# Seven block products in place of eight in both feed-forward parts of a decoder layer

## What is computed

```python
x = x + 1/2 * swiglu(rmsnorm(x), w_gate, w_up, w_down)      # FFN 1
x = x + token_mix(rmsnorm(x))                               # projections, two recurrent mixers, output
x = x + memory_attention(rmsnorm(x), rmsnorm(mem))          # 4 heads over 256 memory tokens
x = x + 1/2 * swiglu(rmsnorm(x), w_gate, w_up, w_down)      # FFN 2
out = rmsnorm(x)
# swiglu(h) = (silu(h @ w_gate) * (h @ w_up)) @ w_down
```

## Time and profile before

| | us |
|---|---|
| runs, median (lowest) | 2969.23 (2969.01) |
| profiled execution, first to last instruction (its own time as the page gives it) | 2967.3 |
| PE busy | 2849.2 (96%) |
| DVE busy | 1354.6 (46%) |
| POOL busy | 1246.7 (42%) |
| ACT busy | 564.3 (19%) |

### The profile page before, as it was taken

One profiled execution on the slowest core, in us unless ns is written; L12 is line 12 of the kernel. 1 busy time (PEld: TensorE's weight loads), 2 busy tenths in 40 slices (PEclk: granted clock), 3 DMA queues, 4 the chain that ended last, 5 costly groups with the idle time before them and its releaser, 6 DMA issues.

```text
span 2967.3 us, 36791 instructions
## 1 busy us (share of the span) xinstructions
PE 2849.2 (96%) x14694; PEld 2359.7 (80%) x14694; DVE 1354.6 (46%) x1109; ACT 564.3 (19%) x793; POOL 1246.7 (42%) x627
## 2 busy tenths in 40 slices
PE   7999999999999998999999999998899999999996
PEld 5888888888788877777777778888788888888885
DVE  5431331234556535776777555543344322331334
ACT  3100010012000112443444232214321100100011
POOL 3433344433694623555555443321043344433331
PEclk9999999999999999998999999999999999999998
DMA  3111111112762554444434164122011111111111
GB/s 133 43 50 50 50 49 45 48 46 103 298 247 92 192 194 149 101 107 139 102 102 104 61 223 149 51 75 102 8 43 50 49 50 47 46 49 50 50 41 73
DMA packets 115401, 271.35 MB, mean 91 GB/s; under 512 B 7644, under 2 KB 58972, under 8 KB 108272
## 3 DMA queue, kind: packets, MB, share of 16 engines
q1 hardware_dynamic: 93504, 210.79, 22.4%
q10 hardware_dynamic: 21808, 59.27, 5.3%
HBM read 207.56 MB, written 62.44 MB: 91 GB/s over the span
## 4 chain that ended last, share of the span: by engine, by line
PE 79%; issue 9%; POOL 6%; DVE 4%; ACT 1%; DMA 0%; SPq 0%; POOLq 0%; DVEq 0%; ACTq 0%
PE G L755 24%; PE G L757 24%; PE G L756 24%; PE G L879 2%; POOL AL L686 2%; PE G L1164 1%; PE G L916 1%; POOL Tr L680 1%; ACT sx L1559 0%; DVE nt_a L1644 0%; DVE mx L2008 0%; DVE px L2016 0%; POOL rho L669 0%; PE G L1156 0%; PE G L820 0%
## 5 line engine op out<-in xcount | busy, mean ns | idle before, releaser
L719 POOL TENSOR_TENSOR whi<-raw,zero 128x1024 fp32r<-128x1024 f32 (+1 forms) x199 | 378.2, 1900 | 1312.8 <-PE G L757 1233.2
L755 PE MATMUL G<-hhi,whi 128*128 128x512 f32 x2032 | 794.0, 391 | 21.0 <-DVE hlo L1650 17.9
L757 PE MATMUL G<-hhi,wlo 128*128 128x512 f32 x2032 | 791.8, 390 | 0.0
L756 PE MATMUL G<-hlo,whi 128*128 128x512 f32 x2032 | 791.5, 390 | 0.0
L722 POOL TENSOR_TENSOR wlo<-raw,whi 128x1024 fp32r<-128x1024 f32 (+1 forms) x199 | 482.6, 2425 | 15.6
L755 PEld LDWEIGHTS G<-hhi,whi 128*128 128x128 f32 x2032 | 382.1, 188 | 104.2 <-issue 13.0
L757 PEld LDWEIGHTS G<-hhi,wlo 128*128 128x128 f32 x2032 | 382.1, 188 | 79.8
L756 PEld LDWEIGHTS G<-hlo,whi 128*128 128x128 f32 x2032 | 382.2, 188 | 79.6 <-issue 0.7
L755 PE MATMUL G<-ahi,whi 128*128 128x512 f32 x960 | 374.8, 390 | 2.7 <-DVEq L457 2.7
L756 PE MATMUL G<-alo,whi 128*128 128x512 f32 x960 | 374.2, 390 | 0.0
L757 PE MATMUL G<-ahi,wlo 128*128 128x512 f32 x960 | 374.1, 390 | 0.0
(11 more groups left out here) (329 smaller groups left out, 3301.8 us busy)
## 6 DMA issues: line engine op xcount, KB each, us to landing
gw<-gw_d SPq DMA_DIRECT2D x32, 1024.0 KB, 5.3
raw<-in_wg SPq DMA_DIRECT2D x44, 512.0 KB, 3.2
raw<-in_wu SPq DMA_DIRECT2D x44, 512.0 KB, 3.3
raw<-in_wd SPq DMA_DIRECT2D x32, 512.0 KB, 3.3
gw_d<-gw SPq DMA_DIRECT2D x16, 1024.0 KB, 4.8
graw<-in_gates_in SPq DMA_DIRECT2D x16, 512.0 KB, 7.2
raw<-in_ml_in SPq DMA_DIRECT2D x16, 512.0 KB, 3.7
zml_d<-po ACTq DMA_DIRECT2D x16, 512.0 KB, 2.6
```

The lines of the kernel that those rows point to most:

```text
L719: nc.gpsimd.tensor_tensor(whi[:, k, 0:w], raw[:, k, 0:w], zero[:].to_broadcast([P, w]), ALU.add).then_inc(hi_made, 1)
L755: nc.tensor.matmul(dst, wh, hi, start=start, stop=False)
L756: nc.tensor.matmul(dst, wh, lo, start=False, stop=False)
L757: return nc.tensor.matmul(dst, wl, hi, start=False, stop=stop)
```

## The change

The product of each feed-forward matrix is cut in 2x2 blocks and taken as seven block products with sums of blocks (a scheme of Strassen's kind) in place of eight.

- **Gate and up.** A unit is now a 256x1024 pair of columns: 11 gate and 11 up units per FFN, each of seven products ("ops") of 4 weight tiles by 512 tokens, 12 matmuls. The seven token operands of FFN entry (`tok`, four blocks or sums of `xT` halves, high and low) are made once and stay on chip. The weight operands are two raw blocks, four sums S1 to S4 and one raw block; POOL makes the four sums and the seven low parts, ACT the seven high parts, through a ring of four slots. ACT copies two partial outputs of a unit out of PSUM (`snap`, `both`); DVE combines the outputs in five steps (C11, v, C22, C12, C21), then scales, and after silu scales again (`gate`, `regate`) and multiplies (`tile`). SP stores finished activations to DRAM (`act_d`).
- **Down.** Product by product in the order 2, 4, 5, 3, 1, 7, 6, each over 11 row pairs (77 ops of 12 matmuls). For an op SP loads one or two weight blocks and, for the first four products, a block of activations from DRAM; POOL adds two weight blocks where the product has a sum (products 1, 2, 5, 6, 7), DVE adds two activation blocks (products 1, 3, 4, 6, 7), ACT makes both high parts, DVE both low parts; DVE also adds finished products onto `xT` (48 results of 128x512), which is loaded again from DRAM, since its place serves as buffer during gate and up.
- **Entry and exit.** Token sums on DVE from copies by ACT; the sum of squares is added on POOL in FFN 1 and on DVE in FFN 2. On exit the squares of even chunks are added by POOL, those of odd ones by DVE.

The diff, cut to its core. The sizes and orders:

```diff
-FF_PARTS = (8, 8, 6)
+FP = FFC // 2
+GU_OPS = 2 * FP * 7
+DN_OPS = 7 * FP
+RING = 4
+GU_WEIGHTS = ("11", "12", "S1", "S2", "S3", "S4", "22")
+DN_ORDER = (2, 4, 5, 3, 1, 7, 6)
+DN_LAG = 15
```

SP, loads and stores of an FFN:

```diff
+        def ffn_io(f):
...
+            for u in range(2 * FP):
+                load_pair(u)
+                if u > 1 and u % 2:
+                    store_tiles((u - 3) // 2)
...
+            for s in range(2 * RING, DN_OPS):
+                load_down(s)
+                p, j = divmod(s - 2 * RING, FP)
+                if p < 3:
+                    sp.wait_ge(dt_lo, f * DN_OPS + s - 2 * RING + 1)
+                    load_block(p + 1, j)
...
+        ffn_io(0)
+        sp.wait_ge(dn_lo, DN_OPS)
         for names, n, tiles, first, u0 in runs():
```

POOL, gate and up, and the first units after FFN 1:

```diff
+            for u in range(2 * FP):
+                low(u, 0)
+                total("S1", u)
+                low(u, 1)
+                total("S2", u)
+                total("S3", u)
+                low(u, 2)
+                total("S4", u)
+                for i in (3, 4, 5):
+                    low(u, i)
+                if f == 0 and u == 0:
+                    for k in range(4):
+                        add_in(k)
+                low(u, 6)
+                if f == 0 and u == 0:
+                    for k in range(4, KD):
+                        add_in(k)
...
+                    if u0 == 0:
+                        pool.wait_ge(op_used, FF_OPS - 5 if r == 0 else FF_OPS)
+                    if u0 == 0 and r == 1:
+                        add_out(0)
                     split(u % 2, i * rounds + u, i + (u // 2 + 1 - aside))
```

PE, one gate or up unit:

```diff
+            for i, bank in enumerate((A, B, C, A, E, B, E)):
+                o = 7 * u + i
+                pe.wait_ge(gu_lo, f * GU_OPS + o + 1)
...
+                if i == 5:
+                    pe.wait_ge(*gu_dve.at("C11", it))
+                if i == 6:
+                    pe.wait_ge(*gu_dve.at("C22", it))
```

ACT, entry to FFN 1:

```diff
+            if f == 0:
...
+                after(1)
+                for k in range(4):
+                    token_square(k)
+                after(2)
+                for k in range(4, KD):
+                    token_square(k)
+                act.wait_ge(in_add, KD + 1)
...
+            for j in range(JP):
+                token_hi(6, j)
```

ACT, exit:

```diff
+            for k in range(0, KD, 2):
+                if gain:
+                    act.dma_start(x_park[:, k, :], xT[:, k, :]).then_inc(store, 16)
+                    activation(hhi[:, k, :], xT[:, k, :], ACT.Copy, scale=v1(gain, k)).then_inc(*out_hi.sig(f"{k}"))
+                square(k)
```

DVE, gate and up:

```diff
+            for u in range(2, 2 * FP):
+                m = u // 2
+                evac("C11", u)
+                evac("v", u)
+                if u % 2:
+                    regate(m, 0)
+                evac("C22", u)
+                if u % 2:
+                    regate(m, 1)
+                evac("C12", u)
+                (tile if u % 2 else gate)(m, 0)
+                evac("C21", u)
+                (tile if u % 2 else gate)(m, 1)
```

DVE, down:

```diff
+            for s in range(DN_OPS):
+                act_sum(s + 1)
+                o = GU_OPS + s
+                dve.wait_ge(op_hi, O + o + 1)
+                tt(ring(wlo, f, o), weight_source(f, o), ring(whi, f, o).bitcast(F32), ALU.subtract).then_inc(dn_lo, 1)
...
+                tt(dtok[:, s % RING, 1, :], src, dtok[:, s % RING, 0, :].bitcast(F32), ALU.subtract).then_inc(dt_lo, 1)
+                if given < len(results) and s >= FP * results[given][0] + DN_LAG:
+                    result(given)
+                    given += 1
```

More of the change, by code:

```diff
@@ new lines, in down @@
+        def down(f, p):
+            for j in range(FP):
+                s = FP * p + j
+                o = GU_OPS + s
+                if j == 0 and p < 2:
+                    pe.wait_ge(*gu_dve.at("C21", f * 2 * FP + 2 * FP - 2 + p))
+                pe.wait_ge(dn_lo, f * DN_OPS + s + 1)
+                pe.wait_ge(dt_lo, f * DN_OPS + s + 1)
+                hi, lo = ring(whi, f, o), ring(wlo, f, o)
+                th, tl = dtok[:, s % RING, 0, :], dtok[:, s % RING, 1, :]
+                for n in range(KD // 2):
+                    if j == 0 and p >= 2:
+                        used = len(DN_OUT[DN_ORDER[p - 2]])
+                        pe.wait_ge(down_out, f * results_before(7) + results_before(p - 2) + used * (n + 1))
+                    bank = down_bank(p, n)
+                    wh, wl = hi[:, n * P:(n + 1) * P], lo[:, n * P:(n + 1) * P]
+                    nc.tensor.matmul(bank, wh, th, start=j == 0, stop=False, skip_group_check=True)
+                    nc.tensor.matmul(bank, wh, tl, start=False, stop=False, skip_group_check=True)
+                    last = nc.tensor.matmul(bank, wl, th, start=False, stop=j == FP - 1, skip_group_check=True)
+                last.then_inc(op_used, 1)
@@ new lines, in ffn, with exit_chunk, exit_norm @@
+        def ffn(f):
+            gate_up(f, 0)
+            pe.wait_ge(consts_in, CONSTS * 16)
+            pe.wait_ge(in_add, (f + 1) * (KD + 1))
+            ones_product(G[1], nt_b[:])
+            for u in range(1, 2 * FP):
+                gate_up(f, u)
+            for p in range(7):
+                down(f, p)
+        def exit_chunk(t):
+            pe.wait_ge(*out_lo.at(f"{t}b" if t % 2 else f"{t}", 0))
+        def exit_norm(f):
+            pe.wait_ge(*out_odd.at("7", f))
+            dve_bank(c.dve)
+            ones_product(bank_dve(c.dve), nt_x[:])
+            c.dve += 1
@@ L1214, in _ @@
         gemm(KD, "dve", hi=ahi, lo=alo)
-        ffn(nt_b[:])
-        norm(nt_b[:], T)
+        ffn(1)
+        exit_norm(1)
     @block.scalar
@@ L1673, in residual @@
             c.advance(unit=KD, dve=KD)
-        def partial(scale):
-            with loop(dve, KD // 2) as i:
-                for r in range(2):
-                    output_ready(i * 2 + (c.unit + r))
-                    x_ = xT[:, i * 2 + r, :]
-                    stt(x_, flat(bank_dve(c.dve + r)[:]), scale, x_, ALU.mult, ALU.add).then_inc(dve_free, 1)
-            c.advance(unit=KD, dve=KD)
         def norm_root(width, ms, r, t):
@@ new lines, in leave, with low @@
+        def leave(f, gain, result):
+            def low(name, k, h0, h1):
+                dve.wait_ge(*out_hi.at(name, 0))
+                stt(hlo[:, k, h0:h1], xT[:, k, h0:h1], v1(gain, k), hhi[:, k, h0:h1].bitcast(F32), ALU.mult,
+                    ALU.subtract).then_inc(*out_lo.sig(name))
+            dve.wait_ge(dt_sum, (f + 1) * sums_before(DN_T, DN_OPS))
+            if gain:
+                for k in range(0, KD, 2):
+                    low(f"{k}", k, 0, T)
+                for k in range(1, KD, 2):
+                    low(f"{k}a", k, 0, HALF)
+            done = results_before(6)
+            result(done)
+            for n in range(1, KD // 2):
+                result(done + n)
+                if gain:
+                    low(f"{2 * n - 1}b", 2 * n - 1, HALF, T)
+            if gain:
+                low(f"{KD - 1}b", KD - 1, HALF, T)
+            for k in range(1, KD, 2):
+                dve.wait_ge(*out_sq.at(f"{k}", f))
+                dve.wait_ge(*(out_odd.at(f"{k - 2}", f) if k > 1 else out_even.at(f"{KD - 2}", f)))
+                tt(nt_x[:], nt_x[:], sqx[:, OUT_SQ.index(f"{k}") % 2, :], ALU.add).then_inc(*out_odd.sig(f"{k}"))
@@ L2146, with quarters @@
     arrays = {}
+    def quarters(w):
+        k, n = w.shape[0] // (2 * P), w.shape[1] // (2 * P)
+        return w.reshape(k, 2, P, n, 2, P)
+    gate_up, down = [], []
     for f in ("ffn1", "ffn2"):
-        n = f[-1]
-        arrays[f"wg{n}"] = units(g[f"{f}_w_gate"][0])
-        arrays[f"wu{n}"] = units(g[f"{f}_w_up"][0])
-        at = 0
-        for part, c in enumerate(FF_PARTS):
-            arrays[f"wd{n}_{part}"] = units(g[f"{f}_w_down"][0][at * P:(at + c) * P])
-            at += c
+        both = np.stack([quarters(g[f"{f}_w_gate"][0]), quarters(g[f"{f}_w_up"][0])], axis=0)
+        gate_up.append(both.transpose(4, 0, 3, 5, 2, 1, 6).reshape(2 * FP, P, 4 * HALF))
+        down.append(quarters(g[f"{f}_w_down"][0]).transpose(0, 2, 4, 1, 3, 5).reshape(FP, P, 4 * HALF))
+    arrays["wgu"] = np.ascontiguousarray(np.stack(gate_up))
+    arrays["wdn"] = np.ascontiguousarray(np.stack(down))
     w_in = g["w_in"][0]
```

761 lines of the change are left out of this document (646 added, 115 removed).

## The result

The changed kernel takes 2944.69 us (median; runs from 2942.55 to 2949.09) where the kernel before takes 2969.25: a ratio of 0.9925, with a 95% interval from 0.9913 to 0.9937. The ratio leaves out the one slow execution of the kernel before (5789.13 us); the two medians give 0.9917. The changed kernel is 25 us faster by the medians, where 77 were forecast. The span of the profiled execution fell from 2967.3 to 2947.3.

What follows compares the result with a forecast made beforehand. PE was taken as the bound, the FFNs by their number of matmuls alone. The saving of 179.4 us and the added costs sum to -77.4: 2967.3 becomes 2889.9, with 1.9 us 2892 us, range 2865 to 2920.

Steps and rivals of the forecast that it cites:

- 792 matmuls: FFN matmuls saved, 396 per FFN, at the measured 0.2265 us each: -179.4 us.
- gate and up, steady: Steady gate and up units: PE stays the bound at 19.03 us per unit; +4 us (0 to +30).
- entry to FFN 1: First unit of FFN 1: tokens of the seventh op wait for POOL's adds of squares; +34 us (22 to 42).
- norm in the second unit: Second FFN unit: root steps and gates on DVE ahead of v and C22; +4 us for both FFNs (0 to 6).
- up to down: From up to down: PE idles behind DVE's last C21, tile and first low parts, twice; +8 us (5 to 12).
- down: loads: Loads in steady down: at most 290 GB/s, under 410; 512 KB lands in 3.3 us, the ring gives 8; no cost.
- down: lock: Down's products 1, 7, 6: DVE instructions on SBUF operands and POOL's exclude each other; +18 us (0 to +66).
- entry to FFN 2: First unit of FFN 2: DVE's work on the last chunks and late weight parts; +14 us (6 to 22).
- exit of FFN 1: Start of rw_in: late raw weights, POOL's squares behind its split, ACT's high parts behind those; +12 us (5 to 18).
- end: Kernel's end: odd squares and sums come behind the even ones, which POOL adds, before the norm's matmul; +8 us (5 to 10).
- Down is bound by the lock: Rival, in down: each DVE instruction excluding POOL's waits for a whole POOL instruction, 66 us; 2940 us, chance 0.17.
- the rival in which POOL's lock bounds them: Gate and up: POOL's eleven instructions make a unit 21.9 us for 19.03; kernel slower, 3015 us, chance 0.08.

Runs made afterwards that it cites:

- e5: Changed kernel with POOL's weight sums in down's last three products (1, 7, 6) cut to 64 of 512 columns: 2929.81 us, ratio 0.9872.
- e1: Changed kernel with the loads of x and the constants asked for one by one behind down's weights of ops 9 to 16: 2921.51 us, ratio 0.9851.
- e9: Changed kernel with e7's exit order, DVE adding all eight squares, and PE taking the even chunks first in rw_in's first unit: 2941.08 us, ratio 0.9903.
- e4: Changed kernel with POOL's sums of even squares ahead of both rw_in weight splits on exit of FFN 1: 2938.92 us, ratio 0.9908.
- e7: Changed kernel with both rw_in splits ahead of POOL's adds, and ACT's high parts ahead of the last two even squares: 2943.46 us, ratio 0.9923.
- e11: Changed kernel with only PE's order of chunks in rw_in's first unit changed, to 0, 2, 4, 6, 1, 3, 5, 7: 2941.15 us, ratio 0.9908.
- e3: Changed kernel with the eight sums of squares on entry to FFN 1 added on DVE in place of POOL: 2936.03 us, ratio 0.9899.
- e6: Changed kernel with the edits of e1, e3 and e7 together: 2911.31 us, ratio 0.9813.
- e10: Changed kernel with the edits of e1, e3 and e9 together: 2911.88 us, ratio 0.9806.
- e12: e10 with the norm's product behind the second unit of rw_in in place of the first: 2907.15 us, ratio 0.9798.
- e13: Changed kernel with the edits of e1, e3, e4 and e11 together: 2910.20 us, ratio 0.9812.

## Why the prediction was wrong

Each term against the trace. A stretch is measured by the starts of PE's ops, less their count of matmuls times 0.2267 us (19.04 us for a unit of 84), and less what the kernel before lost in the same place. The entries go up to the start of the second unit; the norm's four matmuls, which stand there in both kernels, are in both.

| term | forecast | measured |
|---|---|---|
| 792 matmuls | -179.4 | -179.4 |
| gate and up, steady | +4 | 0 |
| entry to FFN 1 | +34 (22 to 42) | +43.0 |
| norm in the second unit | +4 (0 to 6) | +7.5 |
| up to down | +8 (5 to 12) | +10.4 |
| down: loads | 0 | +24.2 |
| down: lock | +18 (0 to 66) | +19.3 |
| entry to FFN 2 | +14 (6 to 22) | +19.1 |
| exit of FFN 1 | +12 (5 to 18) | +27.2 |
| end | +8 (5 to 10) | +8.4, and 0.9 behind it |
| sum | -77.4 | -19.4 (span: -20.0) |

Of the 0.6 us between the sum and the span 0.4 lie in the middle of the kernel; the rest is rounding.

**The number.** The measured 2944.69 us lie above the forecast's own range (2865 to 2920) and within 5 us of the rival "Down is bound by the lock" (2940). That nearness is chance: the lock cost 19.3 us, near the 18 of the forecast, and not the 66 of that rival. Of the prediction's signs of being wrong one appeared, ops of down above 3.4 us, and above all at the start of down (14.71 and 5.26 us), where the forecast had no wait; in products 7 and 6 an op takes 3.0 to 3.2 us on average, and single ones reach 3.5.

**Right.** The saving, and that PE stays the bound in gate and up: each unit takes 19.04 us from the third to the last but one, and the rival in which POOL's lock bounds them needs units over 20.9. Down's lock, by size and place (products 7 and 6 take 33.2 to 35.6 us for 29.9), shown by e5. The end (8.4 for 8), and the step from up to down (10.4 for 8).

**The step that failed: "Loads: at most 768 KB per op in product 5, 290 GB/s, under the 410 of the earlier trace rows; a load of 512 KB lands in 3.3 us, and the ring gives 8."** This counts the steady rate only. It leaves out the 4 MB of x, which the text on the change itself names, the store and the constants, and where they stand in SP's program: between the eighth and the ninth op's weights. No other term is off by as much: these are 24.2 us of the 58 that the sum is off, and e1 brings them back without one byte less.

**The second: the exit of FFN 1, +12.** The mechanism was right (late raw weights, squares behind the split, high parts behind the squares, low parts behind these). The sizes were off. The raw weights landed 7.0 us after their issue, not 3.3, with ACT's stores of x under way in the same stretch (that these are the cause was not tried). The second chunk of `rw_in` came at 26 us after PE's end, not 14, and the last at 29.5, not 20: four of the odd chunks' eight low parts take 2.5 us each, in turns with POOL. And the norm's product came at 38.3, not 25, against which the 12 had been worked out. In e9 it is DVE's own work, in turns with POOL's, that fills the exit to its end. That the same sum of work bounds the changed kernel's exit, rather than its order, is argued and not shown: e4, e7, e9 and e11 brought back 3 to 6 us of the 27.

**Mis-sized: the entries.** In FFN 1 the path was as forecast (DVE and ACT in turns, POOL's adds, tokens of the seventh op), each link late: POOL's adds begin at 51.1, not 44.7, end at 72.5, not 65, and the seventh op starts at 78.95; it and the norm's four matmuls behind it take 5.69 us. In FFN 2 C22 came at 33.7, not 29.4, and the seventh op with the norm took 5.75. PE's waits inside FFN 1's first unit sum to 35.3 us (6.1 + 21.7 + 7.5); up to the start of the second unit it is 45.2 us over its 19.04. Of the other 9.9 the norm's four matmuls are 1.3, and some 8.0 are ops that run, but slowly, at the lower clock, which I had counted for the first op and in part for the last. The fourth op is one of them; its 12 matmuls take 5.22 us in place of 2.72, at a granted clock of 0.50 (columns as in the earlier trace rows):

```profile
46.37:51.59 5.22, 5.22 (x12) 4.10 (x13) 4.81 (x6) 5.22 (x8) 3.06 (x3) 0.50 0.00 0
```

Six smaller overshoots (9.0 at the entry to FFN 1, 3.5 at the norm, 2.4 from up to down, 1.3 for the lock, 5.1 at the entry to FFN 2 and 1.3 at the end) make 22.6 us, the two failed steps 39.4, and gate and up cost 4 less than forecast: that is the 58.0 between -77.4 and -19.4.

Some of the prediction's own sums don't come out. In down, 14 less 5.9 is 8.1, not 8.6, so +16 and not +18; that the lock then cost 19.3 makes the term look better than its sum was. At the exit, 25 less 12.9 is 12.1, not 14. Twelve matmuls at 0.42 us take 5.0 and not 4 us for the first op, which took 4.6. And the earlier trace rows show 349 to 449 GB/s once the loads run, 408 on average, not 414 to 449. None of these moves the forecast by more than 2 us.

## What to carry to other kernels

Where a change brings loads that are needed once, write down the queue's program around them, instruction by instruction: what counts is which urgent load stands behind them, not the mean rate. For work on DVE with two operands in SBUF beside work on POOL, add both engines' times as if they were one engine, as a first estimate. Reordering such work mostly moves a wait: the three other orders and the one smaller program of the exit gave 3 to 6 us of 27, while taking work away gave 15 us in down (e5, whose sums are cut short) and 9 in the entry (e3). And a long wait of PE can cost more than its length, because ops behind it can run at the lower clock: in FFN 1's first unit some 8 us on top of 35.3.

## What was not expected of the hardware

Lock. A low part of 128x512 on DVE, 0.69 us alone in e5, took 1.79 in down's last products of the changed kernel when POOL's sum had begun before it (timeline):

```profile
664.47 1.30 POOL L979 TENSOR_TENSOR wsum<-raw 128x512 f32<-128x512 f32 x1 [1.73 <-DMA raw<-in_wdn]
664.53 1.79 DVE L2473 TENSOR_TENSOR wlo<-wsum,whi 128x512 fp32r<-128x512 f32 x1
```

DVE ends 0.55 us after POOL, half the 1.08 of the earlier trace rows at half the size. The waiting shows here as a longer instruction and not as idle time, so DVE looked 96% busy there (65.61 of 68 us from 656 to 724), and in e5 the same program of DVE has some 15 us to spare.

Clock. The same seventh op of FFN 2 with the norm's four matmuls, and the unit behind it, in the changed kernel and in e11, whose entry to FFN 2 is the same program (windows as above; PE clock in the column behind the engines):

```profile
2265.49:2271.24 5.75, 5.75 (x16) 4.03 (x17) 1.19 (x2) 1.26 (x2) 5.75 (x6) 0.70 0.00 0
2271.24:2295.20 23.96, 21.21 (x86) 16.96 (x85) 13.86 (x10) 11.36 (x14) 19.65 (x13) 0.93 0.13 44
```

```profile
2261.09:2265.20 4.11, 4.11 (x15) 2.89 (x16) 1.18 (x2) 0.75 (x2) 4.11 (x5) 1.00 0.00 0
2265.20:2287.80 22.60, 19.86 (x87) 15.92 (x86) 13.85 (x10) 11.85 (x15) 19.91 (x13) 1.00 0.14 47
```

In the one the granted clock was 0.70 and 0.93 on average over these stretches, a mix of the full level (2.4 GHz) and the half one (1.2 GHz), in the other full throughout. PE's waits ahead were nearly the same, 9.1, 2.8, 2.4 and 1.2 us in the one and 8.9, 2.7, 2.4 and 1.2 us in the other. The difference is 3.0 us, in a stretch whose work hadn't changed. FFN 1's entry has both forms as well (the second unit takes 22.5 to 24.0 us in the runs above). Differences of some 3 us between the times of two profiled executions, such as those among e6, e10, e12 and e13, therefore say nothing by themselves. Why one execution gets the clock earlier than the other is not shown by any run here.
